# Window attention: the value product in 64-column halves, or as full 128 x 512 matmuls

## The chip, the cores and the metric

The kernel runs on one NeuronCore of one Trainium2 chip. The metric is device time in microseconds (us) of one execution. The core has five engines with instruction streams of their own: TensorE (PE, matmuls; its weight loads are listed apart as PEld), VectorE (DVE), ScalarE (ACT), GpSimd (POOL) and SyncE (SP, which here issues all DMA transfers). They wait for each other through semaphores only. SBUF is the on-chip memory with 128 partitions, PSUM the accumulation memory into which TensorE writes, used here as eight banks of 512 f32 per partition.

## The reference, cut to what matters

Two transformer blocks run one after the other over 512 tokens of width 1024 and 256 context tokens. The second one holds, in parallel, a gated recurrence (HGRN) and a windowed attention, whose outputs are merged under two gates. The change is in that windowed attention:

```python
def window_attention(q, k, v, kc, vc, sink):      # 8 query heads, 2 key/value heads, head width 64
    # blocks of 128 queries; a block sees itself, its two neighbours and the 256 context tokens
    s_band = einsum('bkgnqd,bknsd->bkgnqs', qb, kb).astype(float32) * scale
    s_band = where(valid, s_band, NEG_INF)
    s_ctx = einsum('bkgnqd,bksd->bkgnqs', qb, kc).astype(float32) * scale
    p = softmax_with_sink(concatenate([s_band, s_ctx], -1), sink_b).astype(v.dtype)
    o = (einsum('bkgnqs,bknsd->bkgnqd', p[..., :3 * BLOCK], vb)
         + einsum('bkgnqs,bksd->bkgnqd', p[..., 3 * BLOCK:], vc))
```

The last statement is the value product: for each block of 128 queries and each key/value head, the four query heads that share it take a weighted sum of the values. All of this is float32.

## The kernel before, in words

Everything is held transposed, features on the partitions and tokens along the free dimension. Large linear layers split each f32 operand into a rounded high part (fp32r) and a remainder and use three fp32r matmuls (`mm3`); weight panels come in through four slots and are split by ACT (high) and DVE or POOL (low). Products inside the attention are plain f32 matmuls, which the profile shows as two MATMUL records each.

The order of all work is one list of steps made in `plan`. Each engine walks the same list and emits its own part of each step, so that an engine's instructions stand in the order of the list. Banks of PSUM are handed out while the list is walked; `Banks.take` picks them by step number, not by time. Short runs of matmuls whose results nobody reads (`turn_over`, the rows `PS<-CC 128x256`) stand at fixed places of the list.

The window stage (class `Window`) works as follows:

- Step `v` makes the values, transposed, for 768 tokens. Step `vt` turns them with six PE transposes into a two-bank PSUM tile, and ACT copies it to `self.vv`, the array of value vectors: keys on the partitions, then six key blocks `c`, two key/value heads `v`, 64 features `n`.
- Queries and keys are made by `lin`, copied by `raw` and rotated by `rope`. Each `rope` holds one f32 matmul of 512 columns over the full array (`PS<-A,CC 128x512`).
- 32 units follow, one for each block of queries and head. For unit t: `score` (PE, 64 rows of the array), maximum and shift on DVE, `exp` on ACT, sum and reciprocal on DVE, `norm` on POOL, `wt` (PE transposes the probabilities, ACT copies them to `self.wt`).
- After every fourth unit comes `value` for a group g of four heads that share a query block: g = 0..7. It contracts over 4 key blocks (the first and last query block, g = 0, 3, 4, 7) or 5 (g = 1, 2, 5, 6), 36 key blocks in all. For each key block it issues two matmuls, b = 0 and 1: each uses the same 64 value vectors as weights, writes partitions 64b to 64b+63, and streams the two heads of that parity, 256 columns. Partitions are then what the merge needs: even heads below, odd heads above.
- `out` for group g: ACT copies the high part from PSUM to `OAH`, DVE subtracts for the low part in `OAL`; both in two halves of 64 partitions.
- Steps t = 8 to 24 of that loop also carry halves of the gate products of the merge (`half`, twelve 128x512 fp32r matmuls each, `PS<-HT...,RW...`). After t = 24 only the attention's own work and the fill matmuls are left.

The merge follows: its `out` product over the window's result reads `OAL` of all eight groups. The last group is therefore followed by 6 matmuls that need only the first four groups, and then by ones that need group 7. `Ar` in the rows is the stage's work array in its fp32r view, `A` the same array in f32, `TM` a temporary.

Of the kernel before, what the change touches and what calls it, by code (L numbers as in the profile page):

```python
# [2987 lines left out]
class Window(Stage):  # L2988
# [6 lines left out]
    def __init__(self, k, gen):  # L2995
        self.k, self.gen = k, gen
        A, TM = k.A, k.TM
        self.w = k.a["mix_w_in_2"][0]
        at = [8192]

        def al(n):
            at[0] += n
            return A[:, at[0] - n:at[0]]
        self.OAH, self.OAL = (k.AR[:, 4096 + 2048 * i:6144 + 2048 * i].rearrange("p (m t) -> p m t", t=512) for i in range(2))
        early = al(2560)
        self.CO, self.SI, self.raw, self.rt = (early[:, 512 * i:512 * i + 512] for i in range(4))
        self.rr = early[:, 1024:1792]
        self.wt = [x.rearrange("p (x j n) -> p x j n", x=5, j=4) for x in (TM[:, 0:2560], early)]
        self.WM = al(256).rearrange("p (d n) -> p d n", d=2)
        self.q = al(2048).rearrange("p (m t) -> p m t", t=512)  # L3010
        self.kk = al(1536).rearrange("p (m t) -> p m t", t=768)
        self.vv = al(768).rearrange("p (c v n) -> p c v n", c=6, v=2)
        self.es = (al(640), TM[:, 2560:3200], TM[:, 3200:3840], TM[:, 3840:4480])
        self.SK = k.sink
        self.st = tuple(k.dst[:, 8 * i:8 * i + 8] for i in range(3))
        self.units = [(n, 4 * kv + j) for kv in range(2) for n in range(4) for j in range(4)]
# [47 lines left out]
    def tensor(self, p, step, *a):  # L3064
        k, w, hs, ready = self.k, self.w, (self.k.HTH, self.k.HTL), ht_ready(self.k, self.gen)
        if step == "v":
            lin(p, k, Product(("win", "v"), [wp(w, 640, 128)], hs, 8, cover(NT), ready))
        elif step == "vt":
            pv = k.banks.take(p, 2, "win", "vt")
            p.wait_ge("s.win_in", "v")  # L3070
            for c in range(6):
                last = p.tr(pv[:, c * 128:c * 128 + 128], self.rr[:, c * 128:c * 128 + 128])
            last.then_inc("pe.win", "vt")
        elif step == "lin":
            i, part = a
            if part == 0:
                cut = wp(w, 128 * i, 128) if i < 4 else wp(w, 512 + 64 * (i - 4), 64)
                p.win_made = Product(("win", "lin", i), [cut] if i < 4 else [cut, cut], hs, 8, cover(512 if i < 4 else NT),
                                     ready)
                p.win_made.open(p, k)  # L3080
            made = p.win_made
            for kk in range(4 * part, 4 * part + 4):
                for c0, c1 in made.cols:
                    last = made.tile(p, k, c0, c1, kk)
            if part:
                made.close(k, last)
        elif step == "rope":
            i, = a
            pv = k.banks.take(p, 1, "win", "rope", i)
            p.wait_ge("s.win_in", "raw", i)  # L3090
            p.mm(pv[:, 0:512], k.perm, self.raw, True, True).then_inc("pe.win", "rope", i)
        elif step == "score":
            n, h = self.units[a[0]]
            r, kv = slice(64 * (h % 2), 64 * (h % 2) + 64), h // 4
            lq = self.q[r, h // 2, n * 128:n * 128 + 128]
            pv = k.banks.take(p, 2, "win", "score", *a)
            p.wait_ge("v.win_rope", max(h // 2, 1))
            for x, c in self.keys(n)[:-2]:
                at = 128 * x if x < 2 else 512
                p.mm(pv[:, at:at + 128], lq, self.kk[r, kv, c * 128:c * 128 + 128], True, True)  # L3100
            p.mm(pv[:, 640:896], lq, self.kk[r, kv, 512:768], True, True).then_inc("pe.win", "score", *a)
        elif step == "wt":
            n, _ = self.units[a[0]]
            pv = k.banks.take(p, 2, "win", "wt", *a)
            p.wait_ge("g.win_n", *a)
            for x, _ in self.keys(n):
                last = p.tr(pv[:, x * 128:x * 128 + 128], self.es[a[0] % 4][:, x * 128:x * 128 + 128])
            last.then_inc("pe.win", "wt", *a)
        elif step == "value":
            g, = a  # L3110
            n, kv = g % 4, g // 4
            pv = k.banks.take(p, 1, "win", "value", g)
            p.wait_ge("s.win_in", "vt")
            p.wait_ge("s.win_wt", 4 * g + 3)
            keys = self.keys(n)
            for x, c in keys:
                for b in range(2):
                    last = p.mm(pv[64 * b:64 * b + 64, 0:256].rearrange("p (a n) -> p a n", a=2), self.vv[:, c, kv, :],
                                self.wt[g % 2][:, x, :, :].rearrange("p (a b) n -> p a b n", a=2)[:, :, b, :],
                                x == keys[0][0], x == keys[-1][0])  # L3120
            last.then_inc("pe.win", "value", g)

    def scalar(self, s, step, *a):
        k = self.k
        if step == "v":
            s.wait_ge_all("win.start")
            s.wait_ge("pe.lin", "win", "v")
            s.copy(self.rr, k.banks.of("win", "v")[:, 0:NT]).then_inc("s.win_in", "v").frees("win", "v")
        elif step == "vt":
            s.wait_ge("pe.win", "vt")  # L3130
            pv = k.banks.of("win", "vt")[:, 0:NT].rearrange("p (c n) -> p c n", n=64)
            s.copy(self.vv.rearrange("p c v n -> p (c v) n"), pv).then_inc("s.win_in", "vt").frees("win", "vt")
        elif step == "raw":
            i, = a
            pv = k.banks.of("win", "lin", i)
            if i == 4:
                s.wait_ge("pe.win", "vt")
            else:
                s.wait_ge("v.win_rope", {5: 4, 0: 5}.get(i, i - 1))
            s.wait_ge("pe.lin", "win", "lin", i)  # L3140
            if i > 3:
                s.copy(self.kk[:, i - 4, 512:768], pv[:, 512:768])
            s.act(self.raw, pv[:, 0:512], ACT.Copy, scale=0.125 if i < 4 else 1.0).then_inc("s.win_in", "raw", i).frees(
                "win", "lin", i)
        elif step == "exp":
            t, = a
            n, h = self.units[t]
            lo, hi = self.span(n)
            ev, sv, pv = self.es[t % 4], self.st[t % 3], k.banks.of("win", "score", t)
            s.wait_ge("v.win_max", t)  # L3150
            s.act(ev[:, 256:640], pv[:, 512:896], ACT.Exp, bias=sv[:, 2:3], accum_out=sv[:, 3:4]).then_inc(
                "s.win_x", t).frees("win", "score", t)
            s.act(ev[:, lo:hi], ev[:, lo:hi], ACT.Exp, bias=sv[:, 2:3], accum_out=sv[:, 4:5])
            s.act(sv[:, 5:6], self.SK[:, h:h + 1], ACT.Exp, bias=sv[:, 2:3]).then_inc("s.win_e", t)
        elif step == "wt":
            t, = a
            n, _ = self.units[t]
            x0, g = self.keys(n)[0][0], t // 4
            pv = k.banks.of("win", "wt", t)[:, 0:640].rearrange("p (x n) -> p x n", x=5)
            if g == 1:  # L3160
                s.wait_ge("v.win_rope", 3)
            if g > 1:
                s.wait_ge("pe.win", "value", g - 2)
            s.wait_ge("pe.win", "wt", t)
            if n < 3:
                made = s.copy(self.wt[g % 2][:, x0:, t % 4, :], pv[:, x0:, :])
            else:
                s.copy(self.wt[g % 2][:, 0, t % 4, :], pv[:, 0, :])
                made = s.copy(self.wt[g % 2][:, 2:, t % 4, :], pv[:, 2:, :])
            made.then_inc("s.win_wt", t).frees("win", "wt", t)  # L3170
        elif step == "out":
            g, = a
            s.wait_ge("pe.win", "value", g)
            for b in range(2):
                hi, _, pv = self.result(g, b)
                made = s.copy(hi, pv)
            made.then_inc("s.win_oah", g)

    def result(self, g, b):

        n, kv, r = g % 4, g // 4, slice(64 * b, 64 * b + 64)
        pv = self.k.banks.of("win", "value", g)[r, 0:256].rearrange("p (a n) -> p a n", a=2)
        return *(x[r, 2 * kv:2 * kv + 2, n * 128:n * 128 + 128] for x in (self.OAH, self.OAL)), pv

    def vector(self, v, step, *a):
# [745 lines left out]
```

## Time and profile before

| | us |
|---|---|
| Median of 3 runs | 4058.37 |
| Lowest and highest of them | 4054.52, 4064.77 |
| The profiled execution, its own time | 4058.37 |
| Its span, from first to last instruction | 4056.5 |
| PE busy in it | 3846.6 (95% of the span) |
| ACT, DVE, POOL busy | 1428.5, 1609.5, 1185.1 |

The profiled execution took as long as the median, and 1.9 us of it lie outside the span. Matmuls overlap in the pipeline, so that the duration of one is longer than the distance from its start to the next one's start. What a run of matmuls costs the engine is read as start to start. The granted clock of TensorE has two levels, 1.2 and 2.4 GHz; a stretch at 1.00 ran wholly at the upper one.

### The profile page before, as it was taken

How to read it: one execution, taken by the hardware profiler on the slowest of the kernel's cores; microseconds unless marked ns; L12 is line 12 of the kernel's file. 1: busy time of each engine (PE TensorE's matmuls, PEld its weight loads, DVE VectorE, ACT ScalarE, POOL GpSimd, SP SyncE). 2: the span in 40 equal slices, each digit the busy share in tenths (PEclk: the TensorE clock that was granted, in tenths of full speed). 3: DMA queues.
4: the chain of work that ended last, by engine and by line, in shares of the span. 5: the costliest groups of instructions: out<-in, count | busy, mean ns of one | idle time of the engine just before them, and what ended most of it. 6: DMA issues, size and time to landing. Idle time of an engine off the chain costs nothing.

```text
span 4056.5 us, 53819 instructions
## 1 busy us (share of the span) xinstructions
PE 3846.6 (95%) x22755; PEld 3235.2 (80%) x22755; DVE 1609.5 (40%) x2686; ACT 1428.5 (35%) x2312; POOL 1185.1 (29%) x745
## 2 busy tenths in 40 slices
PE   7999889999999999998999999999989989999998
PEld 5777667888887788887888888888877777788887
DVE  4355573111126666656312321011357754432113
ACT  4223343211125424424422432211355536443223
POOL 2011012111123515426322421121433423243224
PEclk9999999999999999999999989999999999999999
DMA  5221133322232121123333422222332211152333
GB/s 180 73 80 32 58 98 116 99 95 94 94 107 85 32 61 45 36 63 107 102 119 104 130 73 67 64 63 63 89 103 59 64 47 37 52 155 75 99 94 109
DMA packets 471978, 336.74 MB, mean 83 GB/s; under 512 B 17609, under 2 KB 445627, under 8 KB 471739
## 3 DMA queue, kind: packets, MB, share of 16 engines
q1 hardware_dynamic: 471056, 333.05, 27.0%
q8 instruction: 180, 2.95, 0.3%
q14 instruction: 59, 0.48, 0.0%
q10 hardware_dynamic: 683, 0.26, 0.0%
HBM read 331.17 MB, written 2.10 MB: 82 GB/s over the span
## 4 chain that ended last, share of the span: by engine, by line
PE 79%; DVE 7%; ACT 5%; POOL 4%; DMA 2%; issue 2%; SPq 0%; ACTq 0%; POOLq 0%; DVEq 0%
PE PS L107 77%; DVE A L124 2%; POOL TM L124 2%; PE PS L115 2%; ACT A L118 1%; POOL RWr L124 1%; ACT L118 1%; ACT RWH L121 1%; POOL A L124 1%; DVE A L132 1%; DMA MW<-in_w_ada 1%; DVE SM L144 1%; DMA MW<-in_mod_w 0%; DVE XT L124 0%; DVE TM L132 0%
## 5 line engine op out<-in xcount | busy, mean ns | idle before, releaser
L124 POOL TENSOR_TENSOR RWr<-RW,RWH 128x1024 fp32r<-128x1024 f32 (+2 forms) x316 | 727.9, 2306 | 2304.2 <-ACT RWH L121 2296.8
L107 PE MATMUL PS<-HTH,RWH 128*128 128x512 f32 (+1 forms) x3360 | 1204.7, 359 | 18.1 <-DVE HTr L124 5.2
L107 PE MATMUL PS<-HTr,RWH 128*128 128x512 f32 (+1 forms) x3360 | 1179.2, 351 | 0.0
L107 PE MATMUL PS<-HTH,RWr 128*128 128x512 f32 (+1 forms) x3360 | 1178.3, 351 | 0.0
L107 PE MATMUL PS<-Ar,RWH 128*128 128x512 f32 (+1 forms) x3264 | 820.3, 342 | 17.6 <-DVE XT L132 7.1
L107 PEld LDWEIGHTS PS<-HTH,RWH 128*128 128x128 f32 x3360 | 643.2, 191 | 132.1 <-issue 36.0
L107 PEld LDWEIGHTS PS<-HTH,RWr 128*128 128x128 f32 x3360 | 642.2, 191 | 84.6 <-issue 0.4
L107 PEld LDWEIGHTS PS<-HTr,RWH 128*128 128x128 f32 x3360 | 643.2, 191 | 80.9 <-issue 2.4
L107 PEld LDWEIGHTS PS<-Ar,RWH 128*128 128x128 f32 x3264 | 564.7, 191 | 105.5 <-issue 15.9
L121 ACT ACTIVATE RWH<-RW 128x1024 fp32r<-128x1024 f32 (+2 forms) x474 | 474.7, 1006 | 315.4 <-DMA RW<-in_ffn_w_out 167.2
L107 PE MATMUL PS<-Ar,RWr 128*128 128x512 f32 (+1 forms) x1632 | 553.2, 339 | 0.0
L124 DVE TENSOR_TENSOR A<-A,PS 128x512 f32<-128x512 f32 (+2 forms) x184 | 133.7, 727 | 827.2 <-PE PS L107 805.8
L124 DVE TENSOR_TENSOR RWr<-RW,RWH 128x1024 fp32r<-128x1024 f32 (+2 forms) x158 | 199.4, 1262 | 605.2 <-ACT RWH L121 605.1
L107 PEld LDWEIGHTS PS<-Ar,RWr 128*128 128x128 f32 x1632 | 312.1, 191 | 33.5
L107 PE MATMUL PS<-A 128*128 128x128 f32 (+5 forms) x1728 | 292.7, 335 | 45.6 <-DVE A L124 19.5
L107 PEld LDWEIGHTS PS<-A 128*128 128x128 f32 (+2 forms) x1728 | 209.7, 192 | 100.4 <-issue 39.5
L121 ACT ACTIVATE Ar<-A 128x512 fp32r<-128x512 f32 (+2 forms) x132 | 91.2, 691 | 552.2 <-DVE A L124 538.1
L118 ACT ACTIVATE A<-PS 128x768 f32<-128x768 f32 (+2 forms) x148 | 92.7, 632 | 527.6 <-PE PS L107 515.5
L132 DVE SCALAR_TENSOR_TENSOR XT<-PS,M,XT 128x512 f32<-128x512 f32 (+1 forms) x200 | 118.0, 618 | 292.3 <-PE PS L107 291.9
L121 ACT ACTIVATE A<-PS 128x256 f32<-128x256 f32 (+5 forms) x207 | 105.8, 534 | 277.9 <-PE PS L107 208.8
L118 ACT ACTIVATE A<-A 128x512 f32<-128x512 f32 (+3 forms) x160 | 105.0, 680 | 237.2 <-DVE A L124 123.9
L118 ACT ACT_TABLE_LOAD x137 | 175.8, 1283 | 31.4 <-PE PS L107 19.0
(195 smaller groups left out, 3934.9 us busy)
## 6 DMA issues: line engine op xcount, KB each, us to landing
RW<-in_ffn_w_in SPq DMA_DIRECT2D x176, 512.0 KB, 3.8
MW<-in_mod_w SPq DMA_DIRECT2D x83, 512.0 KB, 4.7
MW<-in_w_ada SPq DMA_DIRECT2D x72, 512.0 KB, 4.5
RW<-in_ffn_w_out SPq DMA_DIRECT2D x64, 512.0 KB, 3.8
RW<-in_ffn_w_out SPq DMA_DIRECT2D x64, 384.0 KB, 3.3
RW<-in_mix_w_in SPq DMA_DIRECT2D x41, 512.0 KB, 3.8
RW<-in_ssd_w_in SPq DMA_DIRECT2D x40, 512.0 KB, 3.9
RW<-in_ev_w_in SPq DMA_DIRECT2D x24, 512.0 KB, 3.9
```

Source lines behind the costliest of these rows:

```text
L107: return self._ins(self.real and self.real.matmul(o, l, r, start=start, stop=stop, skip_group_check=True))
L115: return self._ins(self.real and self.real.transpose(o, i, self.k.ident[0:n, 0:n]))
L118: return self._ins(self.real and self.real.activation(o, i, f, **kw))
L121: return self._ins(self.real and self.real.activation(o, i, ACT.Copy))
L124: return self._ins(self.real and self.real.tensor_tensor(out=o, in0=i0, in1=i1, op=op))
L132: return self._ins(self.real and self.real.scalar_tensor_tensor(out=o, in0=i0, scalar=sc, in1=i1, op0=op0, op1=op1))
L144: return self._ins(self.real and self.real.reduce_max(o, i, AX.X))
```

## The change

The value product of one key block becomes one matmul. The array `vv` holds each key/value head's 64 value vectors twice, side by side, so that the weights are 128 columns wide. All four heads stream through, 512 columns, and the result fills 128 partitions by 512 columns, one whole bank. Half of it is used: of partitions 0 to 63 the even heads, of partitions 64 to 127 the odd ones; `result` picks them. The second copy in `vv` costs one more ACT copy in step `vt`. `vv` grows by 768 f32 per partition, and the score buffer allotted behind it moves up by as much.

```diff
-        self.vv = al(768).rearrange("p (c v n) -> p c v n", c=6, v=2)
+        self.vv = al(1536).rearrange("p (c v d n) -> p c v d n", c=6, v=2, d=2)
...
             for x, c in keys:
-                for b in range(2):
-                    last = p.mm(pv[64 * b:64 * b + 64, 0:256].rearrange("p (a n) -> p a n", a=2), self.vv[:, c, kv, :],
-                                self.wt[g % 2][:, x, :, :].rearrange("p (a b) n -> p a b n", a=2)[:, :, b, :],
-                                x == keys[0][0], x == keys[-1][0])
+                last = p.mm(pv[:, 0:512], self.vv[:, c, kv, :, :].rearrange("p d n -> p (d n)"),
+                            self.wt[g % 2][:, x, :, :].rearrange("p j n -> p (j n)"), x == keys[0][0], x == keys[-1][0])
...
-            s.copy(self.vv.rearrange("p c v n -> p (c v) n"), pv).then_inc("s.win_in", "vt").frees("win", "vt")
+            for d in range(2):
+                made = s.copy(self.vv[:, :, :, d, :].rearrange("p c v n -> p (c v) n"), pv)
+            made.then_inc("s.win_in", "vt").frees("win", "vt")
...
-        pv = self.k.banks.of("win", "value", g)[r, 0:256].rearrange("p (a n) -> p a n", a=2)
+        pv = self.k.banks.of("win", "value", g)[r, 0:512].rearrange("p (a b n) -> p a b n", a=2, b=2)[:, :, b, :]
```

On PE, at group g = 0 (the transposes of its last unit, the value product, then the scores of the next unit):

```order
 L107 MATMUL PS<-CC 128x256 x3
 L115 MATMUL PS<-CC,A 128x128 x5
-L107 MATMUL PS<-TM,A 64x256 x8
+L107 MATMUL PS<-TM,A 128x512 x4
 L107 MATMUL PS<-A 128x128 x3
 L107 MATMUL PS<-A 128x256
```

Eight matmuls that write 64 partitions become four that write 128, each with twice the columns; nothing around them moves. The same holds at the other seven groups. On PE, at group g = 7 (fill matmuls, the last transposes, the value product, and the first product of the merge):

```order
 L107 MATMUL PS<-CC 128x256 x3
 L115 MATMUL PS<-CC,TM 128x128 x4
-L107 MATMUL PS<-A 64x256 x8
+L107 MATMUL PS<-A 128x512 x4
 L107 MATMUL PS<-Ar,RWH 128x512 x2
 L107 MATMUL PS<-Ar,RWr 128x512
```

Here too only the value product itself differs. On ACT, at step `vt` (the copy of a gate, the copy of the values, the high part of a weight panel, and a copy for `raw`):

```order
 L118 ACTIVATE XT<-PS 128x2x256
-L121 ACTIVATE A<-PS 128x768
+L121 ACTIVATE A<-PS 128x12x64 x2
 L121 ACTIVATE RWH<-RW 128x1024
 L121 ACTIVATE A<-PS 128x256
```

The copy of the values is made twice. The streams of DVE, POOL and SP are the same.

## Rows read from the trace of the kernel before

**Rows 1.** The page, busy time of each engine and the chain that ended last, by engine.
```profile
PE 3846.6 (95%) x22755; PEld 3235.2 (80%) x22755; DVE 1609.5 (40%) x2686; ACT 1428.5 (35%) x2312; POOL 1185.1 (29%) x745
PE 79%; DVE 7%; ACT 5%; POOL 4%; DMA 2%; issue 2%; SPq 0%; ACTq 0%; POOLq 0%; DVEq 0%
```
**Rows 2.** Busy time by stretch: start:end, length, engines (instructions), granted clock, DMA.
```profile
3372.00:3470.00 98.00, 95.33 (x527) 71.09 (x528) 45.54 (x155) 72.77 (x166) 35.91 (x30) 1.00 0.11 33
3470.00:3500.00 30.00, 25.89 (x165) 17.79 (x165) 13.52 (x51) 16.42 (x54) 9.76 (x12) 1.00 0.01 2
3640.00:3660.00 20.00, 17.19 (x133) 13.21 (x133) 6.97 (x14) 8.68 (x18) 7.08 (x6) 0.91 0.43 133
3660.00:3680.00 20.00, 17.49 (x113) 16.88 (x112) 10.39 (x26) 8.82 (x22) 8.21 (x12) 0.83 0.00 1
```
**Rows 3.** PE in order of time: start, us, instruction xrecords [idle before]; groups 0 and 2.
```profile
3376.17 1.95 PE L107 MATMUL PS<-TM,A 128*64 128x256 f32 x16
3378.05 1.37 PE L107 MATMUL PS<-A 64*128 64x128 f32 x8
...
3415.19 2.38 PE L107 MATMUL PS<-TM,A 128*64 128x256 f32 x20
3417.50 1.14 PE L107 MATMUL PS<-A 64*128 64x128 f32 x6
```
**Rows 4.** PE's groups of instructions by shape, 3150 to 3700 us: the value product's.
```profile
L107 PE MATMUL PS<-TM,A 128*64 128x256 f32 x72 | 8.7, 385 | 0.0
L107 PE MATMUL PS<-A 128*64 128x256 f32 x72 | 8.7, 385 | 0.7 <-ACT A L121 0.7
```
**Rows 5.** PE in order of time: one 512-column f32 matmul (two records), and its follower.
```profile
3319.61 1.02 PE L107 MATMUL PS<-A,CC 128*128 128x512 f32 x2
3320.46 1.05 PE L107 MATMUL PS<-CC,SM 128*128 128x128 f32 x8
```
**Rows 6.** The chain that ended last in order of time: start, us, what; groups 1 and 2.
```profile
3394.50 6.58 PE PS L107 x40
...
3415.26 6.37 PE PS L107 x38
```
**Rows 7.** DVE in order of time: the first score after group 5 and after group 6.
```profile
3476.43 0.42 DVE L124 TENSOR_TENSOR TM<-PS,A 128x256 f32<-128x256 f32 x1 [2.21 <-PE PS L107]
...
3489.55 0.29 DVE L124 TENSOR_TENSOR TM<-PS,A 128x128 f32<-128x128 f32 x1 [2.16 <-PE PS L107]
```
**Rows 8.** All engines in order of time: group 7 and what waits for it.
```profile
3497.64 1.95 PE L107 MATMUL PS<-A 128*64 128x256 f32 x16 [0.75 <-ACT A L121]
3499.52 0.73 PE L107 MATMUL PS<-Ar,RWH 128*128 128x512 f32 x2
3499.64 0.77 ACT L121 ACTIVATE Ar<-PS 64x256 fp32r<-64x256 f32 x2 [2.05 <-PE PS L107]
3500.44 0.86 DVE L124 TENSOR_TENSOR Ar<-PS,Ar 64x256 fp32r<-64x256 f32 x2 [5.58 <-ACT Ar L121]
3501.44 0.69 PE L107 MATMUL PS<-Ar,RWH 128*128 128x512 f32 x2 [0.27 <-DVE Ar L124]
```
**Rows 9.** ACT in order of time, at step vt.
```profile
3301.24 0.81 ACT L121 ACTIVATE A<-PS 128x768 f32<-128x768 f32 x1
3301.95 1.05 ACT L121 ACTIVATE RWH<-RW 128x1024 fp32r<-128x1024 f32 x1
3309.64 0.38 ACT L121 ACTIVATE A<-PS 128x256 f32<-128x256 f32 x1 [6.64 <-PE PS L107]
```
**Rows 10.** PE in order of time: the two longest idle times between groups 6 and 7.
```profile
3492.78 0.63 PE L115 MATMUL PS<-CC,TM 128*128 128x128 f32 x4 [1.02 <-POOL TM L124]
...
3496.26 0.63 PE L115 MATMUL PS<-CC,TM 128*128 128x128 f32 x4 [1.56 <-POOL TM L124]
```
**Rows 11.** PE in order of time: a single fp32r matmul of 512 columns, and its follower.
```profile
3382.14 0.39 PE L107 MATMUL PS<-HTH,RWH 128*128 128x512 f32 x1
3382.37 0.40 PE L107 MATMUL PS<-HTr,RWH 128*128 128x512 f32 x1
```

## The prediction

> **What bounds the kernel now.** I read the page's busy times first, then its chain. PE is busy for 95% of the span, and 79% of the chain that ended last is PE [rows 1]. That is a mean over stages, so the next question is what bounds the window stage. Here I read the busy time by stretch. From 3372 to 3470 us, where the halves of the gate products stand between the units, PE is busy for 95.33 of 98 us. From 3470 to 3500 us, where only the attention is left, it is 25.89 of 30 us. The granted clock is 1.00 in both, the 2.4 GHz level [rows 2]. So PE idles for 2.67 + 4.11 = 6.8 us in the whole stretch that holds the eight value products, and none of it for a lower clock. DVE and POOL are busy for less than half of either stretch. ACT, at 72.77 of 98 us, comes nearest.
>
> Then the chain in order of time around the value products. Behind groups 1 and 2 stand pieces of 6.58 and 6.37 us that are PE alone, with the product inside them [rows 6]. In the first stretch whatever makes PE longer makes the kernel longer. In the second the chain leaves PE between the units, through DVE, ACT and POOL, so I had to see who waits for PE behind each late product; that comes below.
>
> **The value product before.** The MATMUL rows of groups 0 and 2 give start to start 3378.05 - 3376.17 = 1.88 us for 16 records and 3417.50 - 3415.19 = 2.31 us for 20 [rows 3]. Group 7 has 3499.52 - 3497.64 = 1.88 again [rows 8]. The difference, one key block with four records, is 0.43 us. All eight: four groups of 4 key blocks and four of 5, so 4 x 1.88 + 4 x 2.31 = 16.8 us. The grouped rows agree: 72 + 72 records, 8.7 + 8.7 = 17.4 us busy, which counts the pipeline's tail of each run too [rows 4].
>
> What is 0.43 us per key block made of? The f32 matmul of 512 columns over the full array in `rope` takes 3320.46 - 3319.61 = 0.85 us, 1.66 ns a column [rows 5]. At that rate one matmul of 256 columns takes 0.427 us. The key block before holds two such matmuls and costs 0.43 us altogether. So the two, which write partitions 0 to 63 and 64 to 127, run beside each other in the two halves of the array's columns. This is the finding on which all else rests. Two half-width matmuls of 256 columns fill the array just as one full-width matmul of 256 columns would.
>
> **The value product after.** One full-width matmul of 512 columns for each key block, the shape, type and size of the `rope` row: 0.85 us [rows 5], of which half goes into results that nobody reads. 36 x 0.853 = 30.7 us. To this comes what a group costs beside its columns. Before, this is 1.88 - 4 x 0.427 = 0.17 us and 2.31 - 5 x 0.427 = 0.17 us [rows 3], or 1.4 us over eight groups. No row shows a full-width f32 product between transposes and scores, so I bound it: 0 if the 0.17 us comes from going into and out of the half-width form, 0.17 us if it belongs to starting and ending any such product. The `rope` row lies at 0. I have no reason to prefer either, since the scores behind, which use 64 rows of the array, stay another form in any case, and I take the middle, 0.7 us for all. The sum is 31.4 us, between 30.7 and 32.1.
>
> Added to PE: 31.4 - 16.8 = 14.6 us, between 13.9 and 15.3.
>
> The Trainium skill, in "TensorEngine Tiling (Array Packing)", section "Tiling Modes", has a rule that speaks for the change: "Changing tiling mode (not just tile) drains the TensorE". By it the product before has a change of mode ahead of it and one behind, and the product after has only the one behind. The trace shows 0.17 us beside the columns and doesn't divide it [rows 3]. By the rule some part of 1.4 us would go, and without it none, so that it moves the sum by less than a tenth and turns nothing round.
>
> **Is it on the path?** Groups 0 to 4 start before 3458 us, in the stretch where PE is at 97% and the chain stays on it [rows 2, 6]; their share passes in full. Behind group 5 DVE waits 2.21 us for the first score, and behind group 6 2.16 us [rows 7]. The score stands on PE behind the product, so it comes later by all that is added, and DVE, then ACT and POOL, have nothing that would hide it. Behind group 7 ACT waits 2.05 us for the product, DVE follows it, and PE, having done the six merge matmuls that need the first four groups, still waits 0.27 us for DVE [rows 8]. The added time moves the product's end, ACT, DVE and that wait alike, and the six matmuls move too. No late group has cover. From there on the merge and the last feed-forward layer keep PE in one line, and I find nothing that takes the delay back.
>
> **The small edits.** The copy in `vt` is made twice. One is 0.81 us (0.71 us to ACT's next start) [rows 9]. The second writes as many elements; bounds 0.7 and 0.8 us. Behind it ACT makes the high part of a panel (1.05 us) and then waits 6.64 us for PE [rows 9]; this idle time hides the copy and the path gets 0. If the cover were gone it would be 0.8 us. The read of PSUM in `out` has the same elements in runs of 128, on the same 64 partitions. No row tells this pattern's price; from 0 to double the four halves (0.77 and 0.86 us a pair, [rows 8]) it is 0 to 1.6 us a group, and in the first seven groups ACT and DVE hold idle time against it. I take 0, because the `vt` copy writes and others read strided tiles at usual prices; for the last group alone 1.6 us is the upper end. The weight loads double in width and lie beside matmuls of 0.43 us a record, longer than before, so 0. No DMA, no bank and no wait changes.
>
> **Sum.** 14.6 us on the span of 4056.5 us gives 4071.1; with the 1.9 us outside it 4073.0 us. The profiled execution's own time is the median of the runs, so no shift is due. Between the bounds: 4072.3 from 13.9, and 4075.3 with 15.3 and the 1.6 of the read. The three runs before lie 10 us apart, and a median can be off by some 4 us.
>
> **Rivals.**
>
> A. *The stage's idle time swallows part of it.* PE idles 6.8 us from 3372 to 3500 [rows 2]; the two longest waits, 1.02 and 1.56 us for POOL [rows 10], lie between groups 6 and 7. If they ended at fixed times, a longer PE would fill them: 14.6 - 6.8 = 7.8 us, 4066.2 us. Against it: these waits end with POOL, which is fed by the scores that stand behind group 6, so they move along. Only waits on work that began ahead of a group can shrink, such as that of a late transpose. I expect under 1 us.
>
> B. *Not slower: a full-width f32 record costs less here than in `rope`.* The place is the 72 MATMUL records left in the eight groups. The sum is 72 x record - 16.8 us, which turns at 0.233 us a record. Below it would go if the array took one column per cycle for these operands as it does for fp32r, where 512 columns take 3382.37 - 3382.14 = 0.23 us [rows 11]: 72 x 0.23 = 16.6 us, and without the 0.17 us a group that stand inside the 16.8 the kernel would be 0.2 us faster, 4058.2 us. Against it: the same engine, shape and type take 0.425 us a record in [rows 5].
>
> C. *The halves did not run beside each other*, and 0.43 us is what a half-width matmul pair costs one behind the other because half the width is cheaper. Then the full-width matmul is still the one of the `rope` row, and the sum stands. It is no rival in time, only in the reason.
>
> D. *The clock.* Behind the window stage there are stretches at 0.91 and 0.83 from 3640 to 3680 us [rows 2]. At 0.83 a third of 20 us ran at 1.2 GHz and lost half of 6.8 us, 3.4 us; at 0.91 it is 1.8 us. A shift of 15 us in what comes ahead may spare these or bring one more of their size: 14.6 + 5.2 = 19.8 us, 4078.2 us, or 14.6 - 5.2, 4067.8 us. Nothing ahead of them changes in kind.
>
> **Chances.** No change can be told from a measurement of this kernel within about 0.3%, 12.2 us: the border lies at 4070.5 us, only 2.5 us below the forecast. The forecast as worked out gets 0.79, of it 0.61 above the border and 0.18 below for the spread of medians. A gets 0.09 (0.08 same, 0.01 slower), D 0.07 (0.05 slower, 0.02 same), B 0.05 (0.03 same, 0.02 faster). In sum 0.67 slower, 0.31 same, 0.02 faster. The range runs from 4065 to 4080 us: A and D at the lower end, D and the upper bound with the spread at the other.
>
> **What would show it.** In the changed profile the value product is 72 records of `128x512`, at 0.85 us for each key block, 3.4 to 3.6 us a group with 4 key blocks and 4.3 to 4.4 with 5, start to start. The score behind each comes later by 1.6 or 2.0 us than now, counted from the group's start. ACT shows two copies of 128x768 at step `vt` with a shorter idle time behind them. PE's busy time grows by about 14 to 15 us, the idle time from the first group to the merge stays near 6.8 us. The forecast is wrong if the record costs other than 0.43 us, if that idle time shrinks by several us, or if PE waits longer behind group 7 for the halves that ACT and DVE read.

## The result, and the profile after

| us | before | changed |
|---|---|---|
| Median of 4 runs | 4056.44 | 4078.36 |
| Lowest and highest | 4053.85, 4064.77 | 4074.12, 4083.49 |
| Profiled execution, its span | 4058.37, 4056.5 | 4084.58, 4082.8 |

The change makes the kernel slower: ratio 1.0051, 95% interval 1.0032 to 1.0070. The medians are 21.9 us apart, where 14.6 us was forecast; 4078.4 us lies 5.4 us above the 4073.0 us of the sum, inside the range given and near its upper end. The profiled execution lies 6.2 us above the median of the changed kernel, so its trace can't be set against the other whole by whole. It is read by stage.

The value product of the changed kernel, PE in order of time (start, us, instruction, number of records), groups 0 and 2, which answer to [rows 3]:

```profile
3384.96 3.60 PE L107 MATMUL PS<-TM,A 128*128 128x512 f32 x8
3388.49 1.37 PE L107 MATMUL PS<-A 64*128 64x128 f32 x8
...
3427.57 4.46 PE L107 MATMUL PS<-TM,A 128*128 128x512 f32 x10
3431.96 1.14 PE L107 MATMUL PS<-A 64*128 64x128 f32 x6
```

Start to start this is 3.53 us for 4 key blocks and 4.39 us for 5, where it was 1.88 and 2.31 us. The difference of the two is 0.86 us a key block, the `rope` row's 0.85 us. All eight groups, if each takes what groups 0 and 2 take: 4 x 3.53 + 4 x 4.39 = 31.7 us. The records by shape, 3150 to 3720 us (busy us, mean ns of one), answer to [rows 4]:

```profile
L107 PE MATMUL PS<-A 128*128 128x512 f32 x36 | 16.2, 595 | 0.7 <-ACT A L121 0.7
L107 PE MATMUL PS<-TM,A 128*128 128x512 f32 x36 | 16.1, 592 | 0.0
```

Half as many records, 32.3 us in place of 17.4. DVE's wait for the first score behind group 5 and behind group 6, which was 2.21 and 2.16 us [rows 7]:

```profile
3495.95 0.42 DVE L124 TENSOR_TENSOR TM<-PS,A 128x256 f32<-128x256 f32 x1 [4.19 <-PE PS L107]
...
3511.04 0.29 DVE L124 TENSOR_TENSOR TM<-PS,A 128x128 f32<-128x128 f32 x1 [4.15 <-PE PS L107]
```

It grew by 1.98 and 1.99 us: nothing hid the added time. Group 7 and what waits for it, which answers to [rows 8]:

```profile
3519.13 3.70 PE L107 MATMUL PS<-A 128*128 128x512 f32 x8 [0.75 <-ACT A L121]
3522.27 1.03 PE L107 MATMUL PS<-Ar,RWH 128*128 128x512 f32 x2
3522.87 0.77 ACT L121 ACTIVATE Ar<-PS 64x256 fp32r<-64x256 f32 x2 [3.79 <-PE PS L107]
...
3523.67 0.86 DVE L124 TENSOR_TENSOR Ar<-PS,Ar 64x256 fp32r<-64x256 f32 x2 [7.32 <-ACT Ar L121]
...
3524.68 0.70 PE L107 MATMUL PS<-Ar,RWH 128*128 128x512 f32 x2 [0.45 <-DVE Ar L124]
```

ACT's wait grew from 2.05 to 3.79 us, by 1.74 us. PE's own wait for DVE grew too, from 0.27 to 0.45 us. The next row of PE shows why: it stands at 3500.08 us before and at 3523.13 us now, 2.44 and 4.00 us behind the product's start. The merge matmuls behind the product come only 1.56 us later, while ACT, which waits for the product's end, comes 1.74 us later, and PE waits for the difference. (The first row behind the product starts after only 3.14 us, but its first matmul then takes longer, 1.03 us for the two where it was 0.73, so that this start can't be read as the product's cost.) The copies and subtractions with the new PSUM pattern take 0.77 and 0.86 us as before.

To measure the stage alone I use two marks that every trace has: the first score (PE has idled 3.2 us there) and the first merge matmul that waits for group 7. The first score before, then that of the changed kernel:

```profile
3345.90 2.04 PE L107 MATMUL PS<-A 64*128 64x128 f32 x6 [3.20 <-DVE A L124]
```

```profile
3354.76 2.04 PE L107 MATMUL PS<-A 64*128 64x128 f32 x6 [3.20 <-DVE A L124]
```

So the stage takes 3524.68 - 3354.76 = 169.92 us. In the kernel before the end is at 3501.44 us [rows 8], and the stage takes 155.54 us. **The stage is 14.4 us longer.** DVE's stream is the same in both, so each of its instructions can be compared with its twin. The distance between twins grows in eight steps, one behind each group: 1.56, 1.97, 2.03, 1.56, 1.57, 1.98, 1.99, 1.74 us, sum 14.4 us. Between these steps it doesn't move by more than 0.06 us at a time. PE's idle time inside the stage stays as it was. The two stretches that answer to the first two of [rows 2] are:

```profile
3381.00:3487.50 106.50, 103.85 (x482) 72.91 (x482) 45.34 (x154) 72.58 (x166) 35.86 (x30) 1.00 0.10 30
3487.50:3522.60 35.10, 31.01 (x136) 18.83 (x136) 13.54 (x51) 16.10 (x53) 9.74 (x12) 1.00 0.00 1
```

That is 2.65 + 4.09 = 6.7 us idle, where it was 6.8 us.

The other 11.9 us between the profiled executions arose outside the stage: the first score itself starts 8.9 us later, and 3.0 us come after the stage. No instruction ahead of the first score differs but the second copy. What else differs in the traces is the granted clock: over 1000 to 2000 us (busy times of PE, PEld, DVE, ACT, POOL, then the clock) of the kernel before, then of the changed one:

```profile
1000.00:2000.00 1000.00, 949.37 (x5957) 806.48 (x5956) 518.52 (x796) 370.89 (x663) 370.09 (x260) 0.99 0.24 73
```

```profile
1000.00:2000.00 1000.00, 954.23 (x5946) 810.14 (x5946) 518.18 (x796) 369.67 (x662) 367.90 (x259) 0.98 0.24 72
```

Nearly the same instructions, and 5 us more of PE at a lower mean clock. Over the whole span the mean granted clock is 0.980 and 0.977. Whether that belongs to the change was open, and became the first experiment.

### The profile page after: what moved, and what is told of

It reads as the page before. It is cut to its first block, busy times and chain, and to the rows that moved or that the text cites. A ratio compares the mean times of both kernels' runs of the same rounds, so it can differ in the third digit from the quotient of the medians.

```text
span 4082.8 us, 53676 instructions
## 1 busy us (share of the span) xinstructions
PE 3876.4 (95%) x22683; PEld 3251.8 (80%) x22683; DVE 1608.8 (39%) x2686; ACT 1428.6 (35%) x2313; POOL 1184.5 (29%) x745
## 4 chain that ended last, share of the span: by engine, by line
PE 79%; DVE 7%; ACT 5%; POOL 3%; DMA 2%; issue 2%; ACTq 0%; SPq 0%; POOLq 0%; DVEq 0%
PE PS L107 78%; DVE A L124 2%; PE PS L115 2%; POOL TM L124 1%; ACT A L118 1%; ACT L118 1%; POOL RWr L124 1%; ACT RWH L121 1%; DVE A L132 1%; DMA MW<-in_mod_w 1%; POOL A L124 1%; DMA MW<-in_w_ada 1%; DVE SM L144 1%; DVE XT L124 0%; DVE TM L132 0%
## 5 line engine op out<-in xcount | busy, mean ns | idle before, releaser
L107 PEld LDWEIGHTS PS<-A 128*128 128x128 f32 (+1 forms) x1692 | 209.7, 193 | 104.3 <-issue 48.5
L121 ACT ACTIVATE A<-PS 128x256 f32<-128x256 f32 (+4 forms) x208 | 106.5, 536 | 277.1 <-PE PS L107 206.4
```

Of the source, the lines that this page charges most:

```text
L107: return self._ins(self.real and self.real.matmul(o, l, r, start=start, stop=stop, skip_group_check=True))
L121: return self._ins(self.real and self.real.activation(o, i, ACT.Copy))
```

## Experiments

The intervals below are of the ratio to the kernel before on the same chip. "Stage" is the time between the two marks, 155.54 us before.

**1. The changed kernel again (after_again).** No edit.

> The changed kernel once more, against the kernel before on the same chip. Its window stage has grown by 14.3 us in the first comparison of traces, the medians of whole runs by 21.9 us. Theory (the extra columns are all of it; the rest is where TensorE's granted clock happened to fall in these runs): the window stage again longer by 14.3 us, the medians apart by 14 to 15 us, and whatever a trace shows beyond that stands outside the window stage and at the lower clock. Rival (the change also makes the rest of the program slower, by 7 to 8 us): the medians again 20 us or more apart.

Measured: ratio 1.0033 (1.0019 to 1.0048), that is 13.4 us, between 7.7 and 19.5. The median of 12 runs (4074.29 us) lies 12.9 us above that of 35 runs before (4061.39 us).

```profile
3345.89 1.80 PE L107 MATMUL PS<-A 64*128 64x128 f32 x6 [3.19 <-DVE A L124]
...
3516.16 0.70 PE L107 MATMUL PS<-Ar,RWH 128*128 128x512 f32 x2 [0.45 <-DVE Ar L124]
```

Stage 3516.16 - 3345.89 = 170.27 us, 14.7 longer. The eight steps are 1.56, 1.99, 1.99, 1.58, 1.56, 1.99, 1.98 and 1.74 us, 14.4 us as in the first trace. The other 0.3 to 0.4 us lies ahead of group 0: the clock is low when the stage starts, and here it stays low until 7.1 us into the stage where it was 6.0 us. The first score now starts at 3345.89 us, as in the kernel before (3345.90). The two spans with their clocks, of the first and of this trace:

```profile
core 0: 4082.8 us, clock 0.977
```

```profile
core 0: 4071.4 us, clock 0.982
```

The theory holds as far as the noise lets one see: the interval leaves out the rival's 20 us, and the stage alone explains the rest. The surplus of the first comparison is not found again. The single runs of the kernel before lie between 4044 and 4075 us, wider than the effect, and they go with the clock: the seven fastest (up to 4052.1 us) have mean granted clocks of 0.982 to 0.985, the seven slowest (from 4067.7 us) 0.976 to 0.979. A straight line through all 35 gives 3.0 us for each 0.001.

**2. The small edits alone (copies_only).** The changed kernel with this product:

```diff
-                last = p.mm(pv[:, 0:512], self.vv[:, c, kv, :, :].rearrange("p d n -> p (d n)"), ...)
+                for b in range(2):
+                    last = p.mm(pv[64 * b:64 * b + 64, 0:512].rearrange("p (a b n) -> p a b n", a=2, b=2)[:, :, b, :],
+                                self.vv[:, c, kv, b, :], ...[:, :, b, :], ...)
```

> The small edits alone: vv doubled and copied twice, PSUM laid out as in the changed kernel and read in runs of 128, but the product still in two half-width matmuls of 256 columns for each key block. Theory (only the matmul's shape costs): the window stage as before within 0.3 us, the time within noise of before. Rival (the strided PSUM write and read, or the second copy, cost): up to 1.6 us a group, 13 us in all, or 0.8 us for the copy.

Measured: ratio 1.0006 (0.9991 to 1.0022). Stage 3503.86 - 3348.09 = 155.77 us, 0.2 longer, all of it ahead of group 0; at none of the eight groups does a DVE instruction shift by more than 0.05 us. The copy, ACT in order of time:

```profile
3303.43 1.51 ACT L121 ACTIVATE A<-PS 128x768 f32<-128x768 f32 x2
3304.82 1.06 ACT L121 ACTIVATE RWH<-RW 128x1024 fp32r<-128x1024 f32 x1
3311.82 0.38 ACT L121 ACTIVATE A<-PS 128x256 f32<-128x256 f32 x1 [5.94 <-PE PS L107]
```

The next instruction starts after 1.39 us in place of 0.71, and the idle time behind shrinks from 6.64 us [rows 9] to 5.94: the second copy is hidden. The strided PSUM write and read cost nothing.

**3. Full width, 256 columns (full_256).** The changed kernel with `pv[:, 0:256]` and the even heads' columns only; the odd heads' product is left out.

> The changed kernel with full-width weights but 256 columns for each key block: only the even heads' probabilities are streamed, so the odd heads' results are left out. It tells what the full width alone costs, and what of the 0.17 us a group belongs to the half-width form. Theory (a full-width matmul of 256 columns takes as long as two half-width ones beside each other): 1.88 us for 4 key blocks, 2.31 us for 5, time as before. By the rule that a change of tiling mode drains the engine: up to 0.17 us a group less, 1.4 us in all.

Measured: ratio 0.9990 (0.9974 to 1.0006). Stage 3508.24 - 3353.65 = 154.59 us, 0.95 shorter, in seven steps of 0.12 to 0.15 us, one behind each group but the last.

```profile
3383.32 0.73 PE L115 MATMUL PS<-CC,A 128*128 128x128 f32 x5 [0.75 <-POOL A L124]
3383.89 1.89 PE L107 MATMUL PS<-TM,A 128*128 128x256 f32 x8
3385.71 1.37 PE L107 MATMUL PS<-A 64*128 64x128 f32 x8
```

1.82 us start to start for 4 key blocks, against 1.88. One full-width matmul of 256 columns takes what the pair of half-width ones took. The rest of the 0.15 us lies ahead of the group: the five transposes before it take 3383.89 - 3383.32 = 0.57 us here, and 3376.17 - 3375.50 = 0.67 us in the kernel before:

```profile
3375.50 0.73 PE L115 MATMUL PS<-CC,A 128*128 128x128 f32 x5 [0.75 <-POOL A L124]
```

**4. One half left out (one_half).** `for b in range(1)` in the kernel before; the odd heads' product is left out.

> The kernel before with only b = 0 of each key block: 36 half-width matmuls of 256 columns, writing partitions 0 to 63. The odd heads' product is left out. Theory (the two halves ran beside each other): a group takes as long as with both, 1.8 us for 4 key blocks and 2.2 to 2.3 us for 5, and the window stage is no shorter than before by more than 0.5 us. Rival (a half-width matmul costs half, and the two ran one after the other): 0.9 to 1.1 us a group, the stage 8 us shorter.

Measured: one run, 4055.22 us; stage 3496.61 - 3340.99 = 155.62 us, 0.1 longer, and no step at any group.

```profile
3371.39 1.94 PE L107 MATMUL PS<-TM,A 128*64 128x256 f32 x8
3373.26 1.37 PE L107 MATMUL PS<-A 64*128 64x128 f32 x8
```

1.87 us with 8 records where 16 took 1.88 [rows 3]. Half the product gone, no time gone: the two halves ran beside each other.

**5. The halves in turn (halves_in_turn).** The kernel before with its two loops exchanged:

```diff
-            for x, c in keys:
-                for b in range(2):
+            for b in range(2):
+                for x, c in keys:
```

> The kernel before with the loops over key blocks and halves exchanged: all b = 0 of a group first, then all b = 1. The same 72 matmuls in another order. Theory (a matmul runs beside its neighbour in the stream only, and only if that uses the other half): but for one pair at the seam they run one after the other, 7 x 0.427 + 0.17 = 3.2 us for 4 key blocks and 9 x 0.427 + 0.17 = 4.0 us for 5, the stage longer by about 12 us. Rival (the engine looks further ahead and starts the other half early): as before.

Measured: ratio 1.0033 (1.0019 to 1.0047). Stage 3531.78 - 3365.55 = 166.23 us, 10.7 longer.

```profile
3395.93 2.86 PE L107 MATMUL PS<-TM,A 128*64 128x256 f32 x16
3398.72 1.37 PE L107 MATMUL PS<-A 64*128 64x128 f32 x8
...
3437.21 3.72 PE L107 MATMUL PS<-TM,A 128*64 128x256 f32 x20
3440.87 1.14 PE L107 MATMUL PS<-A 64*128 64x128 f32 x6
```

2.79 and 3.66 us, a difference of 0.87 us: two matmuls a key block in series, as the theory has it. Both are 0.3 to 0.4 us shorter than expected, so that the seam saves nearly two matmuls and not one. The trace shows why. Three stretches of 0.65 us inside group 0, and one of the same length in the kernel before (busy time of PE, in brackets the records that fall into it, clock):

```profile
3396.19:3396.84 0.65, 0.65 (x4) 1.00 0.00 0
3396.84:3397.49 0.65, 0.65 (x7) 1.00 0.00 0
3397.76:3398.41 0.65, 0.65 (x5) 1.00 0.00 0
```

```profile
3376.64:3377.29 0.65, 0.65 (x8) 1.00 0.00 0
```

The middle stretch is nearly as dense as the halves side by side. The single records start 0.22 us apart until 3396.85 us; there a second sequence sets in beside the first, and the scores follow 3398.72 - 3396.85 = 1.87 us later, as behind the one half of experiment 4. So the second half starts 0.92 us behind the first and not at its end, when three of the first half's eight records are still to start. In the groups with 5 key blocks it sets in after 1.35 us, again with three records left, and 1.35 + 2.31 = 3.66 us. The theory that a matmul runs beside its neighbour in the stream only is too narrow, and the rival is right about the last three records. The eight groups explain 4 x 0.91 + 4 x 1.35 = 9.0 us; 1.6 us more stand between two groups, where the granted clock was low for 3.4 us. Side by side is a matter of the order in the stream, but for a few records at the seam.

**6. Two half-width matmuls of 512 columns (half_512).** The changed kernel with each key block in two matmuls, b = 0 and 1, onto `pv[64 * b:64 * b + 64, 0:512]`.

> The changed kernel's layout and its 512 columns, but in two half-width matmuls for each key block, so 72 of 512 columns. Theory (the cost is the columns streamed through a half, and a pair shares the time): 3.6 us for 4 key blocks and 4.4 us for 5, 0.05 us a group above the changed kernel; the stage longer than before by 14 to 15 us. Rival (full width costs by itself): shorter than that by several us.

Measured: one run, 4070.97 us; stage 3511.71 - 3340.63 = 171.08 us, 15.5 longer.

```profile
3371.10 3.65 PE L107 MATMUL PS<-TM,A 128*64 128x512 f32 x16
3374.68 1.37 PE L107 MATMUL PS<-A 64*128 64x128 f32 x8
```

3.58 us, 0.05 us above the changed kernel's 3.53 us, as expected. Width makes little difference, columns do. The step of the stage behind group 0 is 1.71 us where it was 1.56, so 0.1 us more lies ahead of the product here too, which I had not expected. The first seven groups cost 0.10 to 0.16 us each more than in the changed kernel, 1.0 us in all, and group 7 nothing more: the price of the half-width form that experiment 3 shows, at the other column count. The last 0.2 us of the 15.5 lie ahead of group 0.

**7. Scores in pairs (scores_paired).** In the kernel before the score matmuls use only 64 rows of the array, and two units in a row use different halves. The edit issues them alternately:

```diff
+            if t % 2:
+                return
...
             for x, c in self.keys(n)[:-2]:
                 at = 128 * x if x < 2 else 512
-                p.mm(pv[:, at:at + 128], lq, self.kk[r, kv, c * 128:c * 128 + 128], True, True)
+                for u, pv, lq, r in two:       # units t and t + 1
+                    p.mm(pv[:, at:at + 128], lq, self.kk[r, kv, c * 128:c * 128 + 128], True, True)
```

> The finding turned round. The kernel before, with the scores of two neighbouring units (heads of odd and even number, which stand on partitions 0 to 63 and 64 to 127) issued alternately instead of one unit after the other. Each now uses one half of the array's rows. Theory (halves of the rows run beside each other as halves of the columns do): a pair takes about 1.3 us where two units took 2 x 1.29 us, 16 pairs save up to 19 us; in the stretch without gate products the chain through DVE and ACT gives part of it back. 8 to 19 us faster than before. Rival (only halves of the columns overlap, or the units' PSUM banks come too late): no change, or slower by the waits for two more banks.

Measured: ratio 0.9974 (0.9958 to 0.9991), 10.7 us faster between the medians. Stage 3493.67 - 3349.53 = 144.14 us, 11.4 shorter. A pair:

```profile
3380.71 1.37 PE L107 MATMUL PS<-A 64*128 64x128 f32 x16
3382.01 0.50 PE L107 MATMUL PS<-HTH,RWH 128*128 128x512 f32 x1
```

In the kernel before the first score behind group 0 starts at 3378.05 us [rows 3], and the next row of PE is:

```profile
3379.34 0.77 PE L115 MATMUL PS<-CC,TM 128*128 128x128 f32 x5
```

So two units now take 3382.01 - 3380.71 = 1.30 us, where one took 3379.34 - 3378.05 = 1.29 us. Halves of the rows overlap as halves of the columns do. Part of the gain was lost at two waits:

```profile
3372.43 0.93 PE L115 MATMUL PS<-CC,TM 128*128 128x128 f32 x4 [2.01 <-POOL TM L124]
...
3405.99 0.74 PE L115 MATMUL PS<-CC,TM 128*128 128x128 f32 x5 [2.44 <-issue]
```

Near both the granted clock then fell to 1.2 GHz for 3.4 us, and once more at the end of the stage. Busy time and clock in three stretches of it:

```profile
3345.00:3375.00 30.00, 24.59 (x128) 18.11 (x128) 19.55 (x51) 13.81 (x39) 6.50 (x5) 0.85 0.12 36
3375.00:3455.00 80.00, 77.20 (x472) 57.65 (x471) 39.65 (x137) 64.25 (x146) 34.24 (x29) 0.97 0.13 37
3455.00:3492.00 37.00, 30.14 (x208) 21.13 (x208) 17.70 (x64) 22.45 (x68) 11.43 (x14) 0.95 0.03 8
```

**8. The same with fill at the two waits (paired_fill).**

```diff
-        'Window': {('rope', 1): 6, ('score', 0): 7, ('wt', 4): 3, ...
+        'Window': {('rope', 1): 6, ('score', 0): 7, ('wt', 3): 4, ('wt', 4): 3, ('wt', 10): 5, ...
```

> The kernel with scores in pairs, which made the window stage 11.4 us shorter and not 19, because PE idled at two new places (2.0 and 2.4 us) and the granted clock then fell twice for 3.4 us. Here 4 and 5 fill matmuls of 0.43 us stand ahead of these two waits. Theory (fill in the idle time keeps the clock up and costs nothing): no fall at 3373 and 3407 us, the stage 14 to 15 us shorter than before. Rival (the fills lengthen the waits, or the clock falls elsewhere): 11 us or less.

Measured: median 4042.38 us of 6 runs, ratio 0.9959 (0.9943 to 0.9975), 16.7 us faster than the kernel before; the medians are 17.7 us apart. It has the shortest stage and the lowest median of the study, though its interval overlaps that of experiment 7. Stage 3483.15 - 3342.81 = 140.34 us, 15.2 shorter. The stretches at the same times:

```profile
3345.00:3375.00 30.00, 29.13 (x170) 21.32 (x171) 19.27 (x62) 16.48 (x52) 7.93 (x7) 0.93 0.12 36
3375.00:3455.00 80.00, 77.39 (x474) 58.83 (x473) 39.94 (x137) 66.19 (x146) 32.23 (x27) 1.00 0.14 40
3455.00:3492.00 37.00, 31.82 (x207) 23.30 (x206) 18.83 (x59) 19.45 (x60) 12.57 (x14) 1.00 0.07 19
```

The clock is full from 3375 us on, as the theory said, and the fall that is left in the first stretch is the one behind the first score's wait, which the kernel before has too. The scores' records within the stage, of the kernel before and of this one:

```profile
L107 PE MATMUL PS<-A 64*128 64x128 f32 x160 | 26.7, 296 | 4.5 <-DVE A L124 3.2 <-issue 1.3
L107 PE MATMUL PS<-A 64*128 64x256 f32 x64 | 19.5, 385 | 0.0
```

```profile
L107 PE MATMUL PS<-A 64*128 64x128 f32 x160 | 13.7, 300 | 4.6 <-DVE A L124 3.2 <-ACT TM L118 1.4
L107 PE MATMUL PS<-A 64*128 64x256 f32 x64 | 10.2, 393 | 0.0
```

46.2 us of PE became 23.9. 15.2 of these 22.3 us reached the end.

## Why the prediction was right, step by step

**The two halves ran beside each other.** Right, and the step on which all rested. It was read from 0.43 us a key block against 0.85 us for 512 columns. Experiments 4 (a half left out, no change), 5 (in turn, 0.87 us a key block) and 6 (512 half-width columns, 3.58 us) show it three ways. Rival C is refuted: one half-width matmul of 256 columns alone takes as long as the pair.

**36 x 0.853 us after.** Right: 0.86 us. (The row gives 0.85; its third digit isn't in the rows, and makes 0.1 us of the sum.) Rival B is refuted: a record costs 0.43 us, not 0.23.

**What a group costs beside its columns.** Bounded between 0 and 0.17 us, the middle taken. Of the 0.17 us, 0.05 went with the half-width form (1.88 to 1.82 us in experiment 3, 3.58 to 3.53 us between experiment 6 and the changed kernel). Another 0.1 us went in the transposes ahead of the product, where I had not looked: no term of the sum held it. Together they are 0.15 us at each of seven groups. So what was added is 36 x 0.427 - 7 x 0.15 = 14.3 us, against 14.4 us measured. The forecast took off 0.7 us where 1.05 us goes. That it came so near is in part luck: of the 0.17 us less goes than the half that I took, and the transposes that I had left out make up for it and more.

By the rule in the Trainium skill, "TensorEngine Tiling (Array Packing)", section "Tiling Modes", that a change of tiling mode drains the engine, a group has one such change less. The trace agrees in direction, with 0.15 us a group and the larger part of it ahead of the product. Group 7 has full-width matmuls behind it as well, so there the prediction was wrong to count a change of mode behind the new product. What is saved there isn't on the path, since ACT waits for the product's end.

**The path.** Right at each group: 1.56 to 1.57 us behind groups 0, 3 and 4, 1.97 to 2.03 us behind 1, 2, 5 and 6, 1.74 us behind 7. Rival A is refuted for this stage: PE's waits of 1.02 and 1.56 us in [rows 10] stand in the changed trace with the same lengths, and PE idles 6.7 us where it idled 6.8. One of the signs named for a wrong forecast did show, at a small size: PE waits 0.18 us longer behind group 7. It is the 1.74 us of that group against 1.56 us at the others with 4 key blocks.

**The small edits.** Right at 0 (experiment 2).

**The size.** The term forecast as 14.6 us measured 14.4 us in both traces, step by step, and 13.4 us (7.7 to 19.5) over many runs. The first comparison's 21.9 us holds 7 us that this term doesn't explain. That 4078.4 us still lies in the range is owed to the room that the range leaves for rival D and for the spread of medians, and not to the sum. In the profiled execution the surplus, 11.9 us, lies outside the stage, most of it ahead of it; D had looked for it behind and gave it 5.2 us. A lower granted clock goes with it, 0.977 against 0.980, and by the 35 runs of experiment 1 that would be some 9 us, an estimate. It isn't the whole story: the trace of experiment 1 has 0.982 and yet reaches the first score no earlier than the kernel before. Experiment 1 shows that the surplus doesn't stay. What made it isn't shown, nor is it proved beyond that interval that the change causes none of it.

## What to carry to other kernels

Before replacing two narrow matmuls by a wide one, read start to start whether the pair costs one or two; if the halves already overlap, the wide one only adds columns. Where narrow matmuls use different halves of the rows or columns, issue them alternately: in experiments 5 and 7 order alone cost 10.7 us of stage (1.6 of them where the clock fell) and gained 11.4. When a change shortens a stage by less than the sum, look for new waits and what the clock does behind them; fill matmuls there brought back 3.8 us of stage. And compare traces by the twins of a stream that the change doesn't touch: whole runs that differ by 31 us among themselves could not have shown steps of 0.15 us.

## What I had not expected of the hardware

- The same program differs by more than the effect from one execution to the next: 4044 to 4075 us over 35 runs of the kernel before. Two executions of the changed kernel, with mean clocks of 0.977 and 0.982 over the span, reach the first score 8.9 us apart.
- Going into the half-width form also delays the transposes ahead: 0.67 us for five where the full-width form has 0.57.
- Where the halves follow in turn, the second half starts beside the first when three of its records are left, 0.92 us into a group of 4 key blocks and 1.35 us into one of 5. The seam saves about 0.8 us, nearly two matmuls of 256 columns; I had counted one, 0.43 us.
